# Moving the gate's clip to ScalarE, and the last activation's parts ahead of the last down split, in a mixture-of-experts layer

## What is computed

```python
def expert_block(args):
    x_blk, e = args
    gu = x_blk @ w_gate_up[e] + b_gate_up[e]
    g = jnp.minimum(gu[:, :D_EXPERT], SWIGLU_LIMIT)
    u = jnp.clip(gu[:, D_EXPERT:], -SWIGLU_LIMIT, SWIGLU_LIMIT)
    act = (u + 1.0) * (g * jax.nn.sigmoid(SWIGLU_ALPHA * g))
    return act @ w_down[e] + b_down[e]
```

## Time and profile before

| | us |
|---|---|
| median of 3 runs | 1879.18 |
| lowest, highest | 1879.03, 1880.25 |
| profiled execution, its own time | 1882.29 |
| its span in the trace | 1880.5 |
| PE busy | 1800.9 (96%) |
| DVE busy | 1402.1 (75%) |
| ACT busy | 1231.7 (65%) |

### The profile page before, as it was taken

One profiled execution on the slowest core, in us unless ns is written; L12 is line 12 of the kernel. 1 busy time (PEld: TensorE's weight loads), 2 busy tenths in 40 slices (PEclk: granted clock), 3 DMA queues, 4 the chain that ended last, 5 costly groups with the idle time before them and its releaser, 6 DMA issues.

```text
span 1880.5 us, 53844 instructions
## 1 busy us (share of the span) xinstructions
PE 1800.9 (96%) x21814; PEld 1650.7 (88%) x21814; DVE 1402.1 (75%) x2678; ACT 1231.7 (65%) x1649; POOL 411.4 (22%) x304
## 2 busy tenths in 40 slices
PE   8999998998987999999999999999999999999996
PEld 7777765666876999999999999999999999999996
DVE  5553637775258888888888899999889877757755
ACT  6565327873114777777777788877777776656654
POOL 4000000001003212111112332333122224434433
PEclk9999999999988999999999999999999999999998
DMA  5211101004438988889999999999999999999994
GB/s 153 56 44 39 30 24 45 2 1 142 142 120 295 369 293 308 304 302 320 325 320 322 328 313 343 344 336 345 373 375 365 372 372 374 377 375 372 362 370 134
DMA packets 251408, 479.07 MB, mean 255 GB/s; under 512 B 17312, under 2 KB 38096, under 8 KB 251264
## 3 DMA queue, kind: packets, MB, share of 16 engines
q1 hardware_dynamic: 231040, 443.59, 64.9%
q0 software_dynamic: 20256, 33.94, 7.6%
HBM read 466.96 MB, written 47.19 MB: 273 GB/s over the span
## 4 chain that ended last, share of the span: by engine, by line
PE 50%; issue 6%; DVE 6%; ACT 4%; DMA 2%; DVEq 0%; SPq 0%; POOLq 0%; ACTq 0%; POOL 0%
PE E_p_d L2254 9%; PE E_p_g L2242 5%; PE E_p_g L2245 5%; PE E_p_g L2244 5%; PE E_p_u L2242 5%; PE E_p_u L2245 5%; PE E_p_u L2244 5%; PE E_p_d L2242 3%; PE E_p_d L2245 3%; PE E_p_d L2244 3%; DVE E_w_lo L1996 3%; DMA E_w_st<-in_w_down 2%; PE E_p_t L2180 2%; PE E_p_t L2195 2%; ACT E_w_hi L1869 2%
## 5 line engine op out<-in xcount | busy, mean ns | idle before, releaser
L1996 DVE SCALAR_TENSOR_TENSOR E_w_lo<-E_w_st,E_w_hi 128x2048 f16<-128x2048 f32 x336 | 767.2, 2283 | 31.7 <-ACT E_w_hi L1869 30.5
L1869 ACT ACTIVATE E_w_hi<-E_w_st 128x2048 f16<-128x2048 f32 x336 | 639.0, 1907 | 20.3 <-PEq L1325 16.8
L2242 PE MATMUL E_p_u<-E_x_hi,E_w_hi 128*128 128x128 f16 (+9 forms) x2048 | 366.9, 222 | 1.5 <-DVE E_w_lo L1996 1.4
L2244 PE MATMUL E_p_g<-E_x_lo,E_w_hi 128*128 128x128 f16 (+9 forms) x2048 | 366.9, 222 | 0.5 <-issue 0.5
L2242 PE MATMUL E_p_g<-E_x_hi,E_w_hi 128*128 128x128 f16 (+9 forms) x2048 | 366.9, 222 | 0.0
L2245 PE MATMUL E_p_g<-E_x_hi,E_w_lo 128*128 128x128 f16 (+9 forms) x2048 | 366.9, 222 | 0.0
L2245 PE MATMUL E_p_u<-E_x_hi,E_w_lo 128*128 128x128 f16 (+9 forms) x2048 | 366.8, 222 | 0.0
L2244 PE MATMUL E_p_u<-E_x_lo,E_w_hi 128*128 128x128 f16 (+9 forms) x2048 | 366.8, 222 | 0.0
L1799 POOL DMA_INDIRECT out<-E_y_rows,E_idx_out x66 | 152.6, 2312 | 488.0 <-ACT E_y_rows L1887 467.1
L2242 PE MATMUL E_p_d<-E_a_hi,E_w_hi 128*128 128x160 f16 (+6 forms) x1024 | 210.6, 231 | 6.9 <-DVE E_a_lo L2090 3.5
L2245 PE MATMUL E_p_d<-E_a_hi,E_w_lo 128*128 128x160 f16 (+6 forms) x1024 | 210.5, 231 | 0.0
(11 more groups left out here) (419 smaller groups left out, 3487.2 us busy)
## 6 DMA issues: line engine op xcount, KB each, us to landing
E_w_st<-in_w_gate_up SPq DMA_DIRECT2D x130, 2048.0 KB, 13.5
E_w_st<-in_w_down SPq DMA_DIRECT2D x64, 2048.0 KB, 18.7
A_w_st<-in_w_in SPq DMA_DIRECT2D x20, 512.0 KB, 4.0
A_x_rows<-in_x SPq DMA_DIRECT2D x8, 512.0 KB, 7.9
C_x_res<-in_x SPq DMA_DIRECT2D x8, 512.0 KB, 4.7
x_rows<-C_x SPq DMA_DIRECT2D x8, 512.0 KB, 5.2
out<-C_x SPq DMA_DIRECT2D x8, 512.0 KB, 5.9
h_rows<-C_h SPq DMA_DIRECT2D x8, 512.0 KB, 4.5
```

Source lines behind the costliest of these rows:

```text
L1869: act.activation(w_hi[r][:], staged(c), ACT.Copy, scale=SW).then_inc(hi_s if c < NG else down_hi_s, 1)
L1996: dve.scalar_tensor_tensor(out=w_lo[r][:], in0=staged(c), scalar=SW, in1=w_hi[r][:], op0=ALU.mult, op1=ALU.subtract, accum_out=total[:, c: ...
L2242: pe.matmul(o_, wh, hi[:, k, 0:w], start=h == 0 and k == 0, stop=False, skip_group_check=True)
L2244: pe.matmul(o_, wh, lo[:, k, 0:w], start=False, stop=False, skip_group_check=True)
```

## The change

ACT takes the gate's product itself: with the bias tile now holding S1 x LIMIT less the scaled bias, `Relu(bias - p)` is the limit less the gate, never below zero, and the Silu takes it back by a negative scale and a bias `top` of ALPHA x LIMIT. So `clip_gate` is gone from DVE, and `silu(j)` on ACT is two Relus and one Silu. DVE's reduction to `peak` stands ahead of every split (before: only ahead of those for the next item and the first), and `fold` waits for the splits' own semaphores. Above 128 columns, at c = 7, `activated_hi(3)` and `activated_lo(3)` go ahead of the split of chunk 11, on ACT and on DVE. PE's list, the loads and POOL's transfers are as before (POOL sets `top` once).

```diff
@@ scalar
                     def silu(j):
+                        if j == 0:
+                            act.wait_ge(bias_s, i + 1)
+                        act.wait_ge(gu_mm, NG * i + 2 * j + 1)
+                        if j >= 2:
+                            act.wait_ge(act_s if halves(w) else a_s, NP * i + j - 1)
+                        for h in range(2):
+                            ins = act.activation(gate[j % 2][:, h, 0:w], p_g[j % 2][:, h, 0:w], ACT.Relu,
+                                                 bias=bias[:, 2 * j + h:2 * j + h + 1], scale=-1.0)
+                        ins.then_inc(gate_s, 1)
                         act.wait_ge(gate_s, FREE + NP * i + j + 1)
-                        act.activation(gate[j % 2][:, :, 0:w], gate[j % 2][:, :, 0:w], ACT.Silu, scale=ALPHA / S1
-                                       ).then_inc(silu_s, 1)
+                        act.activation(gate[j % 2][:, :, 0:w], gate[j % 2][:, :, 0:w], ACT.Silu, scale=-ALPHA / S1,
+                                       bias=top[:]).then_inc(silu_s, 1)
...
                         if halves(w):
                             if c >= RING - RI:
                                 act.wait_ge(gu_mm, NG * i + c - (RING - RI) + 1)
+                            if c == NG - 1:
+                                activated_hi(c // 2)
                             if c + RI < NG + n_split(w):
                                 act.wait_ge(w_in[slot(c + RI)], 16 * (i + 1))
                                 split_hi(c + RI, ring(c + RI, w))
-                            if c % 2 == 1:
+                            if c % 2 == 1 and c < NG - 1:
                                 activated_hi(c // 2)
@@ vector
-            def split_lo(k, c, r, first=False):
+            def split_lo(k, c, r):
...
                 dve.wait_ge(hi_s if c < NG else down_hi_s, k)
-                if first:
-                    largest()
+                dve.tensor_reduce(peak[:, c:c + 1], w_hi[r][:, :, 0:1], AX.XY, ALU.max,
+                                  apply_absolute_value=True).then_inc(peak_s if c < NG else down_peak_s, 1)
                 dve.scalar_tensor_tensor(out=w_lo[r][:], in0=staged(c), scalar=SW, in1=w_hi[r][:],
...
-                if not first:
-                    largest()
...
-                dve.wait_ge(peak_s, NG * k)
+                dve.wait_ge(lo_s, NG * k)
+                if wide:
+                    dve.wait_ge(down_lo_s, NP * i + n_split(w))
...
-                    dve.tensor_scalar(bias[:, 0:8], of_expert[:, 0:8], S1, None, ALU.mult)
+                    dve.tensor_scalar(bias[:, 0:8], of_expert[:, 0:8], -S1, S1 * LIMIT, ALU.mult, ALU.add)
...
-                        if c % 2 == 0:
-                            clip_gate(j)
-                        else:
+                        if c % 2 == 1:
                             clip_up(j)
                             product(j)
                         if halves(w):
                             cc = c + RI
+                            if c == NG - 1:
+                                activated_lo(j)
                             if cc < NG + n_split(w):
                                 split_lo(NG * i + cc + 1 if cc < NG else NP * i + cc - NG + 1, cc, ring(cc, w))
-                            if c % 2 == 1:
+                            if c % 2 == 1 and c < NG - 1:
                                 activated_lo(j)
```

33 lines of the change are left out of this document (14 added, 19 removed).

## The result

The changed kernel takes 1903.68 us in the median of 4 runs (1902.57 to 1905.1). The kernel before took 1879.11 on the same chip (4 runs, 1877.44 to 1880.25). The ratio is 1.0123, with a 95% interval from 1.0104 to 1.0142: 24.6 us slower, where 13.7 were forecast, and outside the range of the forecast (1899.0).

What follows compares the result with a forecast made beforehand. PE, busy 96%, bounds the kernel, with weight loads ending beside it at 96 columns. Terms +8.2, +7.1, -1.1 and -0.5 us give +13.7 on the 1879.2 us median: 1892.9 us, range 1885.5 to 1899.

Steps and rivals of the forecast that it cites:

- case A: Expert items: PE waits for x_lo behind the moved split, and DMA holds the tail; 1892.9 us, chance 0.74.
- 144 and 136 columns: Items of these widths: the chain to x_lo delays PE despite the removed a_lo wait; together +7.1 us (4.5 to 9.2).
- I take the middle, 1.6, twice: Two 136-column items: delay between +0.9 (landing early enough) and +2.2 us (landing stays), taken as 1.6 each.
- 184 to 152 columns: Eleven wide items: PE stands for x_lo 0, 0.88 us per 160-column item; together +8.2 us (6.5 to 9.9).
- The step of 0.28 us for eight columns: PE's 84 down matmuls: eight columns less shorten PE's way by 0.28 us, at granted clock 1.00.
- The removed wait for E_a_lo: 136 columns: PE's 1.70 us wait for a_lo 3 goes, as a_lo 3 is there when PE wants it.
- 128 columns: Six items: DVE's relief removes a first-item wait of 0.5 to 0.7 us and small later ones; -1.1 us in all.
- The last ten items: Items of 112 and 96 columns: DVE's relief meets w_down landings, DMA share 1.04; -0.5 us, between 0 and -5.
- B: Tail: the chain is paid, but DMA doesn't hold the tail and DVE's relief counts whole; 1888.4 us, chance 0.10.
- The Relus: Gate clip on ACT: near 0.40 us each, 103 us more ACT work, falling into idle time in wide items.
- D: Items of 144 columns and less: Relu pairs land on the path, 0.67 us, twice per item; 1907 us, chance 0.07.
- The signs it named: Changed kernel's trace: PE waits for E_x_lo about 0.9 us per 160-column item, first-stretch idle about 10 us, no E_a_lo wait.

Runs made afterwards that it cites:

- e5: The whole change plus unread matmuls on PE ahead of turning the second row groups, at 144 and 136 columns; 1900.86 us, ratio 1.0112.
- e6: The whole change, with the next item's slot 5 (down weights 10 and 11) loaded ahead of slots 0 and 1 above 128 columns; 1896.82 us.
- e7: The kernel before, with only half of each down weight loaded from item 23 on; 1880.55 us, ratio 1.0005.
- e8: The clip-alone kernel (e1), with only half of each down weight loaded from item 23 on; 1873.99 us, ratio 0.9966.
- e1: The change without its reordering: clip on ACT, reduction and fold wait kept, chunk 11 split in its old place; 1877.82 us, ratio 0.9987.
- e9: Changed kernel with ACT's old order; only DVE puts low parts of last activation and row groups 0, 1 before chunk 11's split; 1876.43 us.
- e10: e9 plus the early load of slot 5; 1871.81 us, ratio 0.9955.
- e4: Kernel before, clip on DVE, with last activation and row groups 0 and 1 ahead of chunk 11's parts on ACT and DVE; 1883.26 us.

## Why the prediction was wrong, step by step

**The mechanism was right, its cost was not whole.** Direction, place, the engine that waits and the one waited for were those of case A. The step that failed is a term that the sum doesn't have: what the granted clock does behind PE's longer waits. In the items it makes 5.9 us of the 8.9 by which the measured sum (+22.6) is over the forecast (+13.7). The rest is a wide-item term that was 2.5 us too small, 0.7 us at 144 and 136 columns, and two small errors that cancel in part.

**The clock was in no term: 5.9 us, of which 3.7 reach the total.** The forecast said itself that PE would be 2.2 us late at 136 columns on top of what it waited before (1.70 us), so it had waits of 3 to 4 us on paper, and counted only their length. It used the granted clock of 1.00 for waits about twice as long as any under which it had been read: the longest of before in this stage are 1.92 and 1.90 us, and behind 4.36 us the changed kernel's clock is 0.51, and 1.00 only in the second 3.4 us. The rows could not have shown that fall; they could not have excluded it either, and no room was left for it. e5 shows the price apart from the wait (1.10 to 1.29 us for each 3.4 us at half).

**144 and 136 columns: +7.1 forecast, +13.75 measured.** It splits cleanly: the turning of the second row groups came later in its item by 2.17, 1.47 and 0.91 us at 144 columns and by 2.25 and 1.01 at 136, together 7.8, and the half clock added 5.9 behind it. The 7.8 lie inside 4.5 to 9.2, though not item by item: 144 columns were to be 0.9 to 1.6. "I take the middle, 1.6, twice" fits the two items of 136 only as a mean, which is luck: in the first the landing stayed where it was (22.43 us into the item) and the delay was the upper bound; in the second w_hi of chunk 10 started at 21.17, and the delay was near the lower. e6 shows that the landing held the first. And the two parts are not independent: with the clock whole (e5) the landings hold more, and the same five items are +10.1, which is over the 9.2. So this term was also too small for a kernel whose clock had stayed up.

**184 to 152 columns: +8.2 forecast, +10.7 measured.** At 160 columns the path from product 3 to PE took 0.17 us more than the sum has: the wait of the fold for the split's own end was 0.21 us, not the 0.13 read from two short instructions, and a_hi started 0.59 us behind product 3, not 0.52. PE's turning started 0.83 us later instead of 0.72, and the rest of the item took 0.22 more instead of 0.16: 1.05 instead of 0.88, and about as much more (0.17 to 0.25) in each of the nine items, 184 included (0.35 against 0.1). The step of 0.28 us for eight columns is not at fault: in the trace of before the starts of neighbouring matmuls of the f16 parts lie 69.2 ns apart at 160 columns and 65.8 at 152 (means, without the gaps of a wait), and 84 times the difference is 0.28 us. And item 9 already met the landing of slot 5, which the forecast had only from 144 columns on: 1.92 us, of which e6 gives 0.65 back.

**The removed wait for E_a_lo**: gone, as said, and worth nothing with x_lo behind the split.

**128 columns: -1.1 forecast, -0.88 measured.** Right; the first item gave 0.33 and the others 0.11 each.

**The last ten items: -0.5 forecast, -0.95 measured.** The total is near, its parts are not: at 112 columns DVE's relief counted nearly whole (-1.17 us), at 96 it was lost again in item 29. The reason given (the landings do not come earlier when PE does) holds for the items of 96 columns of the changed kernel, as e7 and e8 show, though not for the kernel before, from whose rows it was argued: there the light loads changed nothing. B counted 5.0 us for a tail that DMA doesn't hold; e8 under e7 measured 4.5.

**The Relus: 0.40 us forecast, 388 ns measured** at 160 columns, against 376 ns for DVE's clip; ACT's busy time grew by 80.5 us, not by 103, since neighbours overlap (the 256 Relus cover 80.2 us in the changed kernel, a pair at 160 columns 0.67 us). D does not hold: e1 is faster than before, and in items 11 to 15 by 2.0 us. Its sum is also short by its own words, since "twice per item" in 21 items is 42 pairs and 28 us. The time that D gave, 1907, would have been nearer to the result for the wrong reason.

**The range.** Its two ends don't follow from the terms. The highs add up to 18.5 us, 1897.7, so 1899 is no cut but lies above them, and the lowest sum is 1884.1, not 1885.5. Neither matters for the miss: no term of the sum, at its high, stood for a second effect of a long wait.

**The signs it named** came: PE's transposes waiting for x_lo, PE idle 8.8 us in the first stretch (about 10 forecast), no wait for E_a_lo, ACT waiting 3.3 us for product 3 (2.5 to 3 forecast). One of the items of 96 columns took 34.57 us, just under the 34.6 that was to speak for B, and item 29 took 37.50.

## What to carry to other kernels

Before an instruction is moved ahead of a long one, list what stands behind both on each of the two engines: here the split of 2.3 us was harmless in its old place and held the next item's rows, and through them PE, in its new one, while moving DVE's rows ahead of the split as well (e9) costs nothing, and together with the clip on ACT and an earlier load of the last slot (e10) it gave a kernel 0.45% faster than before (ratio 0.9955). A wait of PE that comes out at over 2 us on paper may cost more than its length: what followed it here was 1.1 to 2.3 us where the clock fell, part of which came back at the next landing that PE would have waited for anyway. And a landing that the trace names beside another releaser may be no bound at all until that other is made faster.

## What the runs showed of the hardware that was not expected

The granted clock of TensorE fell to half behind waits of PE of 2.09, 2.39, 3.18 and 4.36 us in items 11 to 15 of the changed kernel, and stayed there for 3.4 us (three times) or 6.8 us (once); behind a wait of 1.52 us in the same stretch it did not. In no trace of this study did it fall behind a wait under 2.09 us, though there are many between 1.3 and 1.95. The length of the wait doesn't decide alone: with slot 5 early it fell behind 3.08 us and not behind 2.87, with the order alone behind 2.83, 2.50, 3.64 and 3.78 and not behind another of 2.50, and with the rows first not behind two of 2.42, but behind one of 2.41 with DVE clipping (e4). What it depends on beside the wait stays open. Why the stages ahead of the experts take 589 to 596 us from one execution to the next, with the same code, was not looked into; it is about as wide as the spread of the runs of the kernel before (1876.51 to 1885.1 us in 29 runs), while its effect on single runs isn't shown.
